# Ada products in column-grouped units between the weight pieces, their 2 MB transfers begun by GpSimd, in a two-layer decoder step on one core

## The reference, cut to what matters

```python
def layer_forward(x, c, pos, lw, conv_buf, h0, attn_fn):
    ...
    mod = (c @ w_ada_l + b_ada_l).reshape(c.shape[0], N_MOD, -1)
    sh1, sc1, gt1, sh2, sc2, gt2, sh3, sc3, gt3 = [mod[:, m][:, None, :] for m in range(N_MOD)]
    f = swiglu(rms_norm(x, g[0]) * (1 + sc1) + sh1, w_gu[0], w_dn[0])
    x = x + 0.5 * gt1 * rms_norm(f, g[1])
    h = rms_norm(x, g[2]) * (1 + sc2) + sh2
    xl, gl, q, k, v, qi, ki, wi = project(h, w_in_l, pos)
    ...
    y = jnp.concatenate([y_lru, y_att.astype(h.dtype)], axis=-1) @ w_o
    x = x + gt2 * rms_norm(y, g[3])
    f = swiglu(rms_norm(x, g[4]) * (1 + sc3) + sh3, w_gu[1], w_dn[1])
    x = x + 0.5 * gt3 * rms_norm(f, g[5])
```

## Time and profile before

| | us |
|---|---|
| median of 3 runs | 3252.13 (3251.81 to 3252.35) |
| profiled execution, its own time | 3247.81 |
| its span, first to last instruction | 3246.1 |
| TensorE busy (20506 matmuls) | 2854.9 |
| VectorE busy | 1465.4 |
| ScalarE busy | 734.3 |
| GpSimd busy | 158.8 |

### The profile page before, as it was taken

One profiled execution on the slowest core, in us unless ns is written; L12 is line 12 of the kernel. 1 busy time (PEld: TensorE's weight loads), 2 busy tenths in 40 slices (PEclk: granted clock), 3 DMA queues, 4 the chain that ended last, 5 costly groups with the idle time before them and its releaser, 6 DMA issues.

```text
span 3246.1 us, 49665 instructions
## 1 busy us (share of the span) xinstructions
PE 2854.9 (88%) x20506; PEld 2638.2 (81%) x20506; DVE 1465.4 (45%) x2006; ACT 734.3 (23%) x1038; POOL 158.8 (5%) x298
## 2 busy tenths in 40 slices
PE   5999997988778669999979999969796868699997
PEld 4999896976655669999969998969675548699997
DVE  2333124365799443332153331244648992533312
ACT  1222023230012132222222220222200222322221
POOL 0000001001420000000000000010114100000000
PEclk8999998975579789999999999989656889899998
DMA  6232623212353012222243326323124421132231
GB/s 186 83 88 86 183 87 85 73 40 64 115 152 111 20 46 84 86 87 76 87 130 88 89 85 184 90 68 83 48 67 127 141 83 46 39 91 86 71 90 64
DMA packets 524771, 292.75 MB, mean 90 GB/s; under 512 B 20673, under 2 KB 518882, under 8 KB 524162
## 3 DMA queue, kind: packets, MB, share of 16 engines
q1 hardware_dynamic: 513154, 266.35, 28.1%
q0 software_dynamic: 11392, 23.23, 2.4%
HBM read 285.75 MB, written 3.77 MB: 89 GB/s over the span
## 4 chain that ended last, share of the span: by engine, by line
PE 81%; DVE 14%; issue 3%; DMA 1%; ACT 1%; SPq 0%; DVEq 0%; ACTq 0%
PE ps L583 20%; PE ps L581 20%; PE ps L582 19%; PE ps L592 5%; PE ps L703 4%; PE ps L553 3%; DVE sb_arena L1495 3%; PE ps L701 3%; DVE sb_y L1508 3%; PE ps L819 2%; PE ps L563 1%; DMA sb_wslot<-w_ada 1%; DVE sb_h L1122 1%; PE ps L723 1%; DVE sb_h L1149 1%
## 5 line engine op out<-in xcount | busy, mean ns | idle before, releaser
L582 PE MATMUL ps<-sb_h_lo,sb_w_hi 128*128 128x272 f32 x3360 | 972.8, 290 | 0.0
L581 PE MATMUL ps<-sb_h_hi,sb_w_hi 128*128 128x272 f32 x2816 | 817.7, 290 | 54.6 <-DVE sb_h_lo L1135 54.6
L583 PE MATMUL ps<-sb_h_hi,sb_w_lo_ffn 128*128 128x272 f32 x2816 | 820.1, 291 | 0.0
L1110 DVE TENSOR_TENSOR sb_w_lo_ffn<-sb_wslot,sb_w_hi 128x1024 fp32r<-128x1024 f32 (+1 forms) x272 | 324.0, 1194 | 792.3 <-ACT sb_w_hi L874 792.1
L874 ACT ACTIVATE sb_w_hi<-sb_wslot 128x1024 fp32r<-128x1024 f32 (+2 forms) x322 | 332.8, 1036 | 1518.4 <-PE ps L583 1380.0
L582 PEld LDWEIGHTS ps<-sb_h_lo,sb_w_hi 128*128 128x128 f32 x3360 | 640.5, 191 | 0.5
L581 PEld LDWEIGHTS ps<-sb_h_hi,sb_w_hi 128*128 128x128 f32 x2816 | 534.3, 190 | 59.6 <-issue 53.8
L583 PEld LDWEIGHTS ps<-sb_h_hi,sb_w_lo_ffn 128*128 128x128 f32 x2816 | 533.8, 190 | 0.0
L581 PE MATMUL ps<-sb_act_hi,sb_w_hi 128*128 128x272 f32 x1408 | 408.5, 290 | 11.1 <-DVE sb_w_lo_ffn L1110 11.1
L583 PE MATMUL ps<-sb_act_hi,sb_w_lo_ffn 128*128 128x272 f32 x1408 | 407.9, 290 | 0.0
L582 PE MATMUL ps<-sb_act_lo,sb_w_hi 128*128 128x272 f32 x1408 | 407.4, 289 | 0.0
(11 more groups left out here) (217 smaller groups left out, 3152.0 us busy)
## 6 DMA issues: line engine op xcount, KB each, us to landing
sb_wslot<-ffn_w_gu SPq DMA_DIRECT2D x176, 512.0 KB, 3.6
sb_wslot<-w_ada SPq DMA_DIRECT2D x144, 512.0 KB, 4.8
sb_wslot<-ffn_w_down SPq DMA_DIRECT2D x64, 512.0 KB, 3.9
sb_wslot<-w_in SPq DMA_DIRECT2D x32, 512.0 KB, 3.8
sb_wslot<-ffn_w_down SPq DMA_DIRECT2D x32, 384.0 KB, 3.3
sb_down<-key_pages POOLq DMA_DIRECT2D x128, 96.0 KB, 2.2
sb_down<-key_pages SPq DMA_DIRECT2D x128, 96.0 KB, 1.9
sb_wslot<-w_out SPq DMA_DIRECT2D x16, 512.0 KB, 4.1
```

Of the source, the lines that this page charges most:

```text
L581: mm(out, wh, xh, start=(kc == 0), stop=False)
L582: mm(out, wh, xl, start=False, stop=False)
L583: last = mm(out, wl, xh, start=False, stop=(kc == of - 1))
L1110: v.tensor_tensor(w_lo[s][:, 0:rows, 0:cols], wslot[i][:, 0:rows, 0:cols], w_hi[s][:, 0:rows, 0:cols].bitcast(F32), ALU.subtract).then_inc ...
```

## The change

Ada is cut into 36 units of 512 columns (18 a layer), each one transfer of 2 MB. Units 0 to 3 are loaded by SP at the very start and multiplied ahead of layer 0. The other 32 are loaded by GpSimd into one buffer (`ada_w`), each when the unit before has been multiplied, and multiplied between two gate/up pieces, behind every third one in the first block (12 units, from layer 0's unit 4 and from layer 1's unit 4) and behind every sixth one in the second (6 units in layer 0, among them the first four of layer 1, and 2 in layer 1). In a unit four products with the same 32-column `cT` (9 columns padded with zeros) go to four groups of 32 PSUM partitions. VectorE copies the 128 x 128 result out, TensorE transposes it behind the next piece, and VectorE adds the bias. No ada work stands between gate/up and down, in the attention loop or ahead of layer 1.

The splits run over all pieces of both layers in one sequence, two pieces ahead, with three `w_hi` buffers; the low part is written over the slot it came from, so SP loads a slot when TensorE has used the piece four before. Gate/up products go round three pairs of PSUM banks and the fourth pair is left to the units. The sums of squares behind down and the output projection run between the pieces but for the last chunk. Down starts as soon as the first chunks of the activation are ready. All weights lie in DRAM so that a partition's part of a piece is one contiguous row (4 KB; 16 KB of a unit). The gate matrices of a layer come in one transfer instead of 16, the vectors of both layers at the start. The semaphore increments behind waits are gone.

```diff
+UNITS = 18
+UNIT = 512
+UNITS_IN = [[(l * UNITS + 4 + i, 3 * i + 2) for i in range(12)] for l in range(DEPTH)], \
+           [[(l * UNITS + 16 + i, 6 * i + 5) for i in range(6) if l * UNITS + 16 + i < DEPTH * UNITS] for l in range(DEPTH)]
...
-        wslot = [sb(f"wslot{i}", [P, DC, P]) for i in range(RING)]
+        wslot = [sb(f"wslot{i}", [P, DC, P]) for i in range(SLOTS)]
+        w_lo = [nc.alloc_sbuf_tensor_at(f"sb_w_lo{i}", [P, DC, P], F32R, offset=nc.sbuf_base - 4 * DC * P * (SLOTS - i))
+                for i in range(SLOTS)]
+        w_hi = [sb(f"w_hi{i}", [P, DC, P], F32R) for i in range(HIS)]
...
         def _(sp):
-            sp.dma_start(cT[:, :, :], a["cT"]).then_inc(s_in.sem, 16)
-            sp.dma_start(x[:, :, :], a["xT"]).then_inc(s_in.sem, 16)
+            def unit(n):
+                sp.dma_start(ada_first[n].rearrange("p c n -> p (c n)"), a["w_ada"][0, n])\
+                    .then_inc(ada_full0[n].sem, 16)
+            sp.dma_start(cT[:, :, :], a["cT"]).then_inc(c_in.sem, 16)
+            unit(0)
+            sp.dma_start(vecs[:, :, :], a["vec"]).then_inc(s_in.sem, 16)
+            sp.dma_start(states[:, :, :], a["state"]).then_inc(s_in.sem, 16)
+            sp.dma_start(pages[:, :], a["page_table"]).then_inc(s_in.sem, 16)
             sp.dma_start(cst[:, :], a["cst"]).then_inc(s_in.sem, 16)
-            sp.dma_start(pages[:, :], a["page_table"]).then_inc(s_in.sem, 16)
-            sp.wait_ge(s_in.sem, 64)
-            sp.wait_ge(cleared.sem, 1)
+            unit(1)
+            sp.dma_start(x[:, :, :], a["xT"]).then_inc(x_in.sem, 16)
+            unit(2)
+            unit(3)
...
+                def piece(q, src):
+                    rows, cols = shape_of(q)
+                    if q >= SLOTS:
+                        sp.wait_ge(w_used.sem, q - SLOTS + 1)
...
+            def unit(n, pair):
+                buf = ada_first[n] if n < 4 else ada_w
+                if n < 4:
+                    pe.wait_ge(ada_full0[n].sem, 16)
+                else:
+                    pe.wait_ge(ada_full.sem, 16 * (n - 3))
                 for kc in range(DC):
-                    last = mm(ps[0:NC_, bank, i * P:(i + 1) * P], cT[:, kc, :], wslot[i][:, kc, :],
-                              start=(kc == 0), stop=(kc == DC - 1))
-                last.then_inc(ada_used[i].sem, 1)
+                    for g in range(4):
+                        last = mm(ps[32 * g:32 * (g + 1), 2 * pair, 0:P], cT[:, kc, :], buf[:, kc, g * P:(g + 1) * P],
+                                  start=(kc == 0), stop=(kc == DC - 1))
+                last.then_inc(ada_mm.sem, 1)
+            def unit_transpose(n, pair):
+                pe.wait_ge(ada_tok.sem, n + 1)
+                if n:
+                    pe.wait_ge(ada_done.sem, n)
+                nc.tensor.transpose(ps[:, 2 * pair + 1, 0:P], modT[:, :], ident).then_inc(ada_pe.sem, 1)
+            def ffn(l, f):
+                q = l * PIECES + (GU1, GU2)[f]
+                reads = (l * 2 + f) * GU_N
+                units = {n: k for k, n in UNITS_IN[f][l]}
+                for n in range(GU_N):
+                    if n >= 3:
+                        pe.wait_ge(gu_read.sem, reads + n - 2)
+                    piece(q + n, 1 + n % 3, h_hi, h_lo, norm=2 * f if n == 0 else None)
+                    if n - 1 in units:
+                        unit_transpose(units[n - 1], 0)
+                    if n in units:
+                        unit(units[n], 0)
+                q = l * PIECES + (DN1, DN2)[f]
+                for n in range(DN_N):
+                    m, j = divmod(n, len(DN_K))
+                    k0 = sum(DN_K[:j])
+                    if m == 0:
+                        pe.wait_ge(act_ready.sem, act_ready.at(l, f * FC + k0 + DN_K[j]))
...
+                    piece(q + n, dn_pair(m), act_hi, act_lo, k0, FC)
+                    if m and j == 1:
+                        squares_of(m - 1, dn_read, l, f * DC)
+                squares_of(DC - 1, dn_read, l, f * DC).then_inc(ss_ready.sem, 1)
...
             for l in range(DEPTH):
                 l_[0] = l
-                ada(l, ADA0, 0, 2)
+                if l == 0:
+                    for n in range(4):
+                        unit(n, n % 3)
...
                 sums_of_squares(sq_ready, l, 0)
-                ffn(l, 0, GU1, DN1, lambda: ada(l, ADA1, 2, 5))
-                sums_of_squares(dn_read, l, 0)
+                ffn(l, 0)
...
                     if i and hd == 3:
-                        pe.wait_ge(ada_read.sem, ada_read.at(l, 5 + i))
                         output(i - 1)
-                    if hd == 0 and i:
-                        pe.wait_ge(yt_read.sem, yt_read.at(l, i - 1))
-                        ada_transposes(l, 5 + i - 1, 1)
-                    if hd == 4:
-                        pe.wait_ge(modT_ready.sem, modT_ready.at(l, 2 * (5 + i) + 1))
-                    ada_chunk(l, ADA2, i * RPF, hd, 0)
...
+            def units(l, f):
+                for n, _ in UNITS_IN[f][l]:
+                    if n > 4:
+                        pool.wait_ge(ada_mm.sem, n)
+                    if f:
+                        pool.wait_ge(h_parts.sem, h_parts.at(l, 3 * DC))
+                    pool.dma_start(ada_w.rearrange("p c n -> p (c n)"), a["w_ada"][n // UNITS, n % UNITS])\
+                        .then_inc(ada_full.sem, 16)
             for l in range(DEPTH):
+                units(l, 0)
                 key_loads(pool, False, l, 0)
...
                 nc.gpsimd.partition_all_reduce(mxa, mx, P, RMAX).then_inc(pool_max.sem, 1)
+                units(l, 1)
...
+                def unit_token(n, pair):
+                    dve.wait_ge(ada_mm.sem, n + 1)
+                    v.tensor_copy(modT[:, :], ps[:, 2 * pair, 0:P]).then_inc(ada_tok.sem, 1)
+                def unit_bias(n, pair):
...
-                    if hd == 4:
-                        ada_half(5 + i, 0, ADA2, i * RPF + 1, 0)
-                    if i and hd == 0:
-                        ada_half(5 + i - 1, 1, ADA2, i * RPF, 0)
-                    if i and hd == 2:
-                        ada_bias(5 + i - 1, 1)
```

More of the change, by code:

```diff
@@ L68, with dn_pair, shape_of @@
 ST_H, ST_C, ST_ALL = 0, LC * NSEQ, LC * NSEQ * 4
-RING = 4
-RPF = DC // RING
-U_GU = FC // 2
+SLOTS, HIS = 4, 3
+GU_N, DN_N, OUT_N = 2 * FC, 3 * DC, DC
 DN_K = (8, 8, 6)
[L78 to L120, removed]
+GU1 = 0
+DN1 = GU1 + GU_N
+IN = DN1 + DN_N
+OUT = IN + PC + 1
+GU2 = OUT + OUT_N
+DN2 = GU2 + GU_N
+PIECES = DN2 + DN_N
+UNITS = 18
+UNIT = 512
+UNITS_IN = [[(l * UNITS + 4 + i, 3 * i + 2) for i in range(12)] for l in range(DEPTH)], \
+           [[(l * UNITS + 16 + i, 6 * i + 5) for i in range(6) if l * UNITS + 16 + i < DEPTH * UNITS] for l in range(DEPTH)]
+def dn_pair(m):
+    return 1 + (m - 1) % 2 if m else 3
+def shape_of(q):
+    n = q % PIECES
+    if DN1 <= n < IN or n >= DN2:
+        return DN_K[(n - (DN1 if n < IN else DN2)) % len(DN_K)], P
+    return DC, LAST if n == OUT - 1 else P
 PAGE_UNROLL = 4
-ARENA = FC * T + 2048
+ARENA = 13928 + 88
 KREC = PAGE + PAGE // 2
-DVE_STEPS = 361
 class Signal:
@@ L162, in need @@
     def need(self, n):
-        self.eng.wait_ge(self.sem, self.layer * self.per + (n + self.shift))
-    def need_hold(self, n):
-        hold(self.eng, self.passed, self.sem, self.layer * self.per + (n + self.shift))
+        self.eng.wait_ge(self.sem, n)
     def link(self, ins):
         self.need(self.mark(ins))
[L173 to L186, removed]
 def decoder(nc, a):
@@ L565, in product, with piece @@
                 return last
[L567 to L572 removed]
+            def piece(q, pair, hi, lo, k0=0, of=DC, norm=None):
+                rows, _ = shape_of(q)
+                wh, wl = w_hi[q % HIS], w_lo[q % SLOTS]
+                pe.wait_ge(w_split.sem, q + 1)
                 for b in range(2):
[L574 to L578 removed]
+                    for r in range(rows):
+                        if norm is not None and b == 0 and r % 2 == 0:
+                            pe.wait_ge(h_parts.sem, h_parts.at(l_[0], norm * DC + r + 2))
+                        kc = k0 + r
@@ L1050, in _ @@
                 squares_of_x(l, 4)
[L1051 to L1052 removed]
                 root(l, 4)
                 gain_and_shift(l, 2, 6)
[L1055 removed]
+                ffn(l, 1)
                 root(l, 5)
@@ L1209, in ada @@
-                def ada(ph, first, after):
-                    for g in range(first, after):
-                        for half in range(2):
-                            ada_half(g, half, ph, g * RPF + (half + 1 - first * RPF), half)
-                        ada_bias(g, 2)
-                    dve.wait_ge(ada_read.sem, ada_read.at(l, after))
-                hold(dve, passed[3], vec_full.sem, vec_full.at(l, 2))
-                ada(ADA0, 0, 2)
-                pre_norm(0, 0, 1, 0, h_hi, GU1, w_lo_ffn)
```

558 lines of the change are left out of this document (241 added, 317 removed).

## The result

The changed kernel takes 3167.69 us (median of four runs, 3163.65 to 3169.75), the kernel before 3252.24 beside it: ratio 0.9738, 95% interval 0.9721 to 0.9755. That is 84.6 us less; 57.8 were forecast, and the time lies in the range, 0.7 us above its lower end of 3167.

What follows compares the result with a forecast made beforehand. TensorE bounds the kernel, with 81% of the chain in a 3246.1 us span. Removed 146.8, less 9.0 for moved sums and 80 for units, gives 57.8: span 3188.3, median 3194, range 3167 to 3270.

Steps and rivals of the forecast that it cites:

- Four column groups at once: In a unit, four column groups of the array run side by side: 1.74 us plus 0.75, 2.5 a unit; chance 0.62.
- ada between gate/up and down: First feed-forward block of both layers: TensorE's ada work between the two stages goes, 49.3 and 48.2, gaining 97.5 us.
- ada at the head of layer 1: Between layer 0's last down and layer 1's next stage: the ada work goes, 61.23 against 41.5 us, gaining 19.7.
- gate/up to down, second block: TensorE's 3.87 us stand for the split behind the last activation goes in both layers, gaining 7.7 us.
- attention loops: Ada copies, last chunk and waits leave the loops VectorE leads: about 6.7 us a layer, 13.4 in all; increments 0.
- start: Ahead of layer 0's gate/up: earlier transfers let its first matmul start at 65 us, gaining 8.5, between -5.5 and 13.5.
- first pieces at half clock: Half-clock steps at the start of down: nothing priced, a possible gain of 0 to 5 us.
- sums moved: Sums of squares behind down and output product run between pieces: 6.4 us cost, 4.9 gained, at six places, losing 9.0.
- 32 units: Ada units added to the gate/up stages: 2.5 us each, band 1.9 to 3.4, costing 80 us.
- One sign of being wrong: Gate/up: the prediction is wrong if pieces of the same 48 matmuls run longer than 6.0 us beside units.
- The in-order rival: In a unit, a group's second pass must precede the next group's first: 4.25 us a unit, about 3250; chance 0.17.
- The fifth unit's place: At the start, GpSimd's 2.1 MB load beside SP's queue: transfers take 42 us with it, 36 without.

Runs made afterwards that it cites:

- group by group: The changed kernel with a unit's loops over groups and products swapped, all eight products of a column group ahead of the next group's: 3303.3 us, 1.0159 of the kernel before.
- when doubled: The changed kernel with GpSimd loading each of the 32 units twice in a row into the same buffer: 3178.6 us, 0.9780 of the kernel before.

## Why the prediction was right, and where its sizes were off

Four column groups at once was the forecast case, with a chance of 0.62, and it is what the runs show. That the time lies in the range at all is in part luck: two of the four runs (3163.65 and 3166.57) lie below its end of 3167. That end was to be the sum with units at 1.9 and start and clock at their best, which gives 3165 (3194 - 19.2 - 5 - 5). The terms, forecast and measured between the first and last matmuls of the stages:

| step | forecast us | measured us |
|---|---|---|
| ada between gate/up and down | 97.5 | 49.3 + 48.2 = 97.5 |
| ada at the head of layer 1 | 19.7 | 23.9 less 5.0 for its sums = 18.9 |
| gate/up to down, second block | 7.7 | 2 x 4.03 = 8.1 |
| attention loops | 13.4 | 7.6 + 6.7 = 14.3 |
| start | 8.5 | 73.55 to 61.83 = 11.7 |
| first pieces at half clock | 0 | 7.2 at down, -3.1 elsewhere = 4.1 |
| sums moved | -9.0 | 30.8 behind, -36.5 inside = -5.7 |
| 32 units | -80 | 32 x 2.17 = -69.4 |
| rest: pieces of layer 1 at 6.03 for 5.97, loop ends | 0 | -1.5 |
| sum | 57.8 | 78.0 |

**The units** are the largest miss. Four at once was right to 0.2 us (1.98 for 1.74); the 0.75 beside it for the change of form, fill and transpose measured 0.43 with what is above 1.74, and no run shows how that divides. The break-even that the prediction gave, 4.3 us, has runs on both sides: 2.17 gains 2.6%, 6.17 and 7.39 lose; a straight line between the first two gives 4.7, an estimate. One sign of being wrong was set too tight: pieces longer than 6.0 us beside units. A plain piece takes 6.04 before and after, and the two behind a unit 6.17 (with the transpose) and 6.10.

**The in-order rival and the evidence against it.** The score products of the earlier trace rows were read as contradicting the Trainium skill, TensorE: Matmul & The Clock Gate, "Part 3: Packing small matmuls — row/col tiling", by which matmuls keep program order in start and end. That reading, on which the expectation for group by group rests too, was wrong: both products started together and ended together, in order, and the change's records (0, 7, 14, 20, then 134, 140) keep that order too, product by product. The rule did not forbid four at once, so it was no ground for 4.25 us a unit. What does contradict it is the run group by group, where, as the records were read there, a product started 0.21 us ahead of the one before it in the program.

**The loop** came out right by the wrong split. The increment was given 0 (bounds 0 to 5 a layer) and measured 3.2 and 3.5 by the searches; the ada work, given 13.4, then brought about 7.5.

**The half clock at the start of down** was named and not priced. Its first piece takes 6.04 us where it took 7.63, 8.51, 7.61 and 7.62. The windows of before show the clock that was granted in the first piece, and in the next stretch:
```profile
393.84:401.50 7.66, 7.66 (x49) 7.66 (x50) 0.99 (x1) 0.00 (x0) 0.00 (x0) 0.78 0.47 137
401.50:407.50 6.00, 6.00 (x51) 6.00 (x49) 0.96 (x1) 0.85 (x1) 0.00 (x0) 1.00 0.24 70
```
Ahead of it TensorE had paused for 1.67 us; now it comes straight from gate/up. In the second blocks, with no ada work ahead, it had paused for 3.87 us, and the first pieces were as long (8.51 and 7.62 us); so the pause is what all four have in common, though no run tries it by itself. The 7.2 us exceed the bound of 5. In turn, the first pieces of other stages are up to 1.6 us longer, which was not foreseen. Since the same pieces differ by up to 2 us between runs whose edits lie elsewhere, the -3.1 of one profile is not settled.

**The start** moved faster than the 338 GB/s taken from one transfer. The slices of the first 62 us, 1.55 each:
```profile
GB/s 0 233 254 412 412 374 436 475 423 444 413 455 414 438 425 423 443 425 423 433 412 455 423 365 423 423 283 19 0 0 0 0 0 0 0 0 0 0 0 0
```
Most stand at 412 to 455. So the last unit was there at 38.3 us and not at 40, and its products, transposes and copies took 2.9 us and not 4. The Trainium skill, DMA: Bandwidth & Descriptors, "Anatomy of one DMA — SWDGE (gpsimd) path", fits 436 GB/s for the bytes of a transfer behind a fixed 2 us; the slices, which are mostly SyncE's transfers, agree with the rate. For a unit the fit gives an estimate of 6.8 us; beside the pieces' transfers it took 8.2. The fifth unit's place was listed (42 or 36 us) and cost the 5.06 that the run shows.

**The sums** were right in the price of four, 0.91 us inside a stage (0.92 forecast), and in the 4.8 to 5.4 gained behind (4.9); the output stage holds six sums inside and not seven, since the seventh, like the eighth, stands behind the last piece. **Transfers** beside gate/up cost nothing, as priced, and 1.1 us in all when doubled. The 20 us by which the span beat the sum are the units' 10.6, the clock's 4.1, the start's 3.2 and the sums' 3.3, with the rest at -1.0; the other 6 lie in the medians, which stood 6.0 above the span before and 0.4 below it after.

## What to carry to other kernels

Products with 32 columns paid by the column group here: go round the groups product by product, since a group that was issued as a whole kept the next one waiting but for its last two products, and the same move without going round lost more than the move had won. Price work by the engine that leads where it is put: 2.17 us between the weight pieces, about 0.3 us by the searches (0.6 by the attention stages) in a loop that VectorE leads, if no wait of TensorE's is put ahead of what VectorE needs next. Small orders count there as well: the increments in a step, of which one shows on VectorE's chain, were worth half of what the loop gained.

## What the runs showed of the hardware that was not expected

In the run group by group, as its records were read, TensorE started a product ahead of one that stood before it in the program (1340 ahead of 1552 ns), beside the last two products of the group ahead and no earlier, which hid 0.41 us at each change of group. In the loops of the changed kernel the granted clock is 0.50, half speed, where it was 0.83 with ada products between the earlier trace rows, and the loop is still shorter, since VectorE leads. Seven microseconds of products in a single column group left the clock at 1.00 and the next piece at its usual length.
